# Experts' rows: scaled ahead of the scatter and added in memory, in place of eight stored rows per token

## What is computed

```
_, e_idx = lax.top_k(jnp.where(expert_mask, biased, -jnp.inf), TOP_K)
gate = jnp.take_along_axis(scores, e_idx, axis=1)
gate = gate / jnp.sum(gate, axis=-1, keepdims=True) * ROUTED_SCALE
...
yb = lax.map(expert_block, (xin, block_expert)).reshape(n_rows, d)
routed = jax.ops.segment_sum(yb * row_gate[:, None], row_tok, num_segments=T + 1)[:T]
shared = (jax.nn.silu(hf @ sh_gate) * (hf @ sh_up)) @ sh_down
return (routed + shared).reshape(b, s, d)
```

## Time and profile before

| | us |
|---|---|
| median of 3 runs | 3164.0 (3163.98 to 3166.07) |
| the profiled execution | 3163.8 |
| its span, first to last instruction | 3162.2 |
| TensorE busy | 3057.7 (97%) |
| VectorE busy | 1856.5 (59%) |
| ScalarE busy | 561.5 (18%) |
| GpSimd busy | 245.3 (8%) |
| moved by DMA | 566.57 MB |

### The profile page before, as it was taken

One profiled execution on the slowest core, in us unless ns is written; L12 is line 12 of the kernel. 1 busy time (PEld: TensorE's weight loads), 2 busy tenths in 40 slices (PEclk: granted clock), 3 DMA queues, 4 the chain that ended last, 5 costly groups with the idle time before them and its releaser, 6 DMA issues. The chain is left out here.

```text
span 3162.2 us, 39915 instructions
## 1 busy us (share of the span) xinstructions
PE 3057.7 (97%) x12530; PEld 1759.4 (56%) x12531; DVE 1856.5 (59%) x3939; ACT 561.5 (18%) x1282; POOL 245.3 (8%) x377
## 2 busy tenths in 40 slices
PE   7999999999999899999998898999999999999998
PEld 4765667644437433333333444478844688588543
DVE  6766676666537644334333567665557755665667
ACT  1002222210002122222221225410000233200000
POOL 1000000011100122222222100000000000000000
PEclk9999999999999999999999999999999999999999
DMA  7673232378762479999997521122254334122342
GB/s 224 198 225 95 66 100 60 107 252 274 242 227 100 149 310 384 378 390 402 370 369 274 214 80 54 41 74 102 85 186 160 100 81 134 54 100 80 135 184 106
DMA packets 270692, 566.57 MB, mean 179 GB/s; under 512 B 27017, under 2 KB 162804, under 8 KB 245994
## 3 DMA queue, kind: packets, MB, share of 16 engines
q1 hardware_dynamic: 213712, 413.72, 36.9%
q0 software_dynamic: 46992, 140.43, 12.7%
q10 hardware_dynamic: 9866, 10.82, 1.0%
HBM read 554.22 MB, written 36.83 MB: 187 GB/s over the span
## 5 line engine op out<-in xcount | busy, mean ns | idle before, releaser
L1522 PE MATMUL ps<-WR,hT 128*64 x832 | 373.7, 603 | 22.8 <-issue 20.7
L1523 PE MATMUL ps<-WR,hT 128*64 128x512 f32 x832 | 373.7, 603 | 0.0
L1967 PE MATMUL ps<-WR 128*128 128x512 f32 x784 | 337.4, 592 | 1.0 <-DVEq L3572 0.7
L1522 PEld LDWEIGHTS ps<-WR,hT 128*64 128x64 f32 x832 | 115.2, 139 | 264.9 <-issue 264.9
L1967 PEld LDWEIGHTS ps<-WR 128*128 128x128 f32 x784 | 148.6, 190 | 188.9 <-issue 186.0
L1161 PE MATMUL ps<-hT,WR 128*128 128x512 f32 x512 | 225.5, 596 | 0.6 <-DVE WR L2813 0.6
L3284 DVE COPY WR<-WR 128x1024 f32 x208 | 131.0, 693 | 160.4 <-SPq L756 110.6
L1926 PE MATMUL ps<-WR 128*128 128x256 f32 x960 | 217.0, 379 | 0.0
L1926 PEld LDWEIGHTS ps<-WR 128*128 128x128 f32 x960 | 182.4, 190 | 24.8
L1543 PE MATMUL ps<-WR 128*64 x416 | 189.5, 598 | 2.7 <-DVEq L3297 1.8
L1544 PE MATMUL ps<-WR 128*64 128x512 f32 x416 | 189.7, 598 | 0.0
(11 more groups left out here) (483 smaller groups left out, 4699.3 us busy)
## 6 DMA issues: line engine op xcount, KB each, us to landing
WR<-in_w_gate SPq DMA_DIRECT2D x64, 1024.0 KB, 8.4
WR<-in_w_up SPq DMA_DIRECT2D x64, 1024.0 KB, 10.8
WR<-in_w_down SPq DMA_DIRECT2D x64, 1024.0 KB, 9.9
WR<-in_mlp_w SPq DMA_DIRECT2D x56, 1024.0 KB, 6.8
WR<-in_mlp_w SPq DMA_DIRECT2D x20, 2048.0 KB, 8.4
xr<-in_ada_w POOLq DMA_DIRECT2D x32, 1024.0 KB, 5.6
WR<-in_w_in SPq DMA_DIRECT2D x56, 512.0 KB, 7.0
xr<-in_w_ada POOLq DMA_DIRECT2D x16, 1024.0 KB, 5.6
```

Source lines behind the costliest of these rows:

```text
L1522: mm(out[0:HALF], xT[u][:, k, 0:HALF], wa[:, :, k, :], start=(k == 0), stop=(k == KD - 1))
L1523: last = mm(out[HALF:P], xT[u][:, k, HALF:P], wb[:, :, k, :], start=(k == 0), stop=(k == KD - 1))
L1967: return mm(ps[:, bank, :], rows, weights, start=(row == 0), stop=(row == PAST[phase] - 1))
```

## The change

Each expert's row is multiplied by its gate on the way out of PSUM: `turn_y` takes a scale per row, `gate_c[u]`. The gates of a turn's rows come by one more indirect gather of 128 single numbers from a small array in DRAM, `gate_dram`, which GpSimd writes once ahead of the loop from `gate8`; `pair_i` holds the row numbers for it. The scatter then adds in memory (`compute_op=ALU.add`) to one of four sums per token: by turn parity u (two arrays `y_sums[u]`) and by half of the turn (`half_c` adds 512 to the row number in the upper half). Both arrays are filled with zeros from an input `blank` while the program is still ahead of the routing. The combine stage loads four row tiles per token tile in place of eight, into sixteen places of their own, so that the loads wait for nothing but the last scatters. TensorE adds all four by products with the identity, the shared expert of three tiles goes ahead of the waits, and VectorE reads the sum straight from PSUM. The sixteen products of identity and gate on ScalarE are gone. In the residual of this stage VectorE now does all four `branch_in` first and the four `gained` behind them.

```diff
+        y_sums = [nc.dram_tensor(f"y_sum{u}", (2 * T, D), F32, kind="Internal").ap() for u in range(2)]
+        gate_dram = nc.dram_tensor("gate_dram", (T * PER_TOKEN, 1), F32, kind="Internal").ap()
...
+            for u in range(2):
+                pool.dma_start(y_sums[u].rearrange("(r p) d -> p r d", p=P), blank.unsqueeze(1).to_broadcast(
+                    [P, 2 * TT, D])).then_inc(sem("y_blank"), 16)
...
-            def put(u, column, n):
+            def put(u, column, n, more=True):
...
+                if more:
+                    pool.tensor_copy(pair_c[u].bitcast(I32), pair_i[:, bass.ds(column, 1)].bitcast(I32)).then_inc(
+                        sem("put_c"), 1)
...
+                if more:
+                    pool.indirect_dma_start(gate_c[u], None, gate_dram,
+                                            bass.IndirectOffsetOnAxis(ap=pair_c[u].bitcast(I32), axis=0),
+                                            bounds_check=T * PER_TOKEN - 1, oob_is_err=False).then_inc(
+                                                sem(f"gate_in{u}"), 16)
+                pool.indirect_dma_start(y_sums[u], bass.IndirectOffsetOnAxis(ap=put_c[u].bitcast(I32), axis=0),
+                                        ybuf[u], None, bounds_check=2 * T - 1,
+                                        oob_is_err=False, compute_op=ALU.add).then_inc(sem(f"y_out{u}"), 16)
...
+            pool.wait_ge(sem("route_v"), ROUTE_V["gates"])
+            pool.dma_start(gate_dram.rearrange("(t p j) o -> p t (j o)", p=P, j=PER_TOKEN), gate8).then_inc(
+                sem("gates_out"), 16)
+            pool.wait_ge(sem("gates_out"), 16)
+            pool.wait_ge(sem("y_blank"), 32)
...
+            for t in range(TT):
+                for i in range(ACC):
+                    pool.dma_start(y_in[t][i], y_sums[i // 2][(i % 2) * T + t * P:(i % 2) * T + (t + 1) * P, :]).then_inc(
+                        sem(f"y_in{t}"), 16)
...
+            def ffn_rows(t):
+
+                pe.wait_ge(sem(f"y_in{t}"), 16 * ACC)
+                for i in range(ACC):
+                    for n in range(2):
+                        last = mm(ps[:, 2 * t + n, :], ident[:, :], y_in[t][i][:, 512 * n:512 * n + 512],
+                                  start=False, stop=(i == ACC - 1))
...
+                act.wait_ge(sem(f"gate_in{u}"), (h >> 1) * 16 + 16)
+                A(ybuf[u], ps[:, 5:7, :].rearrange("p b c -> p (b c)"), ACT.Copy, scale=gate_c[u]).then_inc(
+                    sem("moe_y_free"), 1)
...
+            link.mark(V.memset(half_c[0:HALF, :], 0.5 - PER_TOKEN / 2))
+            link.mark(V.memset(half_c[HALF:P, :], 0.5 - PER_TOKEN / 2 + T * PER_TOKEN))
+            for u in range(2):
+                link.mark(V.memset(gate_c[u], 0.0))
...
+            link.mark(V.tensor_copy(pair_i.bitcast(I32), pair))
...
             def combined(t):
...
+                dve.wait_ge(sem("ffn_p"), t + 1)
+                return ps[:, 2 * t:2 * t + 2, :].rearrange("p b c -> p (b c)")
```

More of the change, by code:

```diff
@@ L131 @@
 ROUTE_P = dict(router_p=1, counts_p=2, ranks_p=3, ends_p=4, first_p=5, tiles_p=6, table_p=7, rows_p=8)
-ROUTE_V = dict(chosen=1, before=2, sums=3, starts=4, ends=5, slots=6, tile_e=7, onehot=8, stack=8 + TT, row_i=9 + TT)
+ROUTE_V = dict(chosen=1, before=2, sums=3, starts=4, ends=5, slots=6, tile_e=7, onehot=8, stack=8 + TT, row_i=9 + TT, gates=10 + TT)
 ADA_SHORT = dict(sum=4 + 1, p=1, free=2, into=(0, 0), bufs=2)
@@ L310, with program @@
 ]
-def program(nc, a, onehot, counting, out):
+def program(nc, a, onehot, counting, blank, out):
     ctx = ExitStack()
@@ L476, in program @@
         fold = view(R, 20588, TURNS)
+        pair_i = view(R, 20460, TURNS)
+        pair_c = [view(R, 20524 + i, 1) for i in range(2)]
+        gate_c = [view(R, 20526 + i, 1) for i in range(2)]
+        half_c = view(R, 20528, 1)
         gate8 = view(R, 18724, TT, PER_TOKEN)
@@ L526, in program @@
         modx = view(R, 19968, 9 * ADA_C)
-        yg = [view(R, D * i, D) for i in range(YG)]
-        gate_diag = view(R, 16384, TT * PE_ROWS, P)
+        y_in = [[view(R, D * (ACC * t + i + (1 if t == TT - 1 else 0)), D) for i in range(ACC)] for t in range(TT)]
         ada0 = [view(R, 512 * i, 512) for i in range(4)]
@@ L1580, in ffn_rows @@
                     for k in range(FE):
-                        last = mm(ps[:, 2 * t + n, :], hexp[k][:, t * P:(t + 1) * P], w[:, k, 512 * n:512 * n + 512],
-                                  start=(k == 0), stop=False)
-                last.then_inc(sem("ffn_p"), 1)
[L1584 to L1591, removed]
+                        mm(ps[:, 2 * t + n, :], hexp[k][:, t * P:(t + 1) * P], w[:, k, 512 * n:512 * n + 512],
+                           start=(k == 0), stop=False)
+            def ffn_rows(t):
[4 more added lines that the diff above has]
+                                  start=False, stop=(i == ACC - 1))
+                last.then_inc(sem("ffn_p"), 1)
             have("sh_down", 0)
+            for t in range(TT - 1):
+                shared_rows(t)
             for t in range(TT - 1):
@@ L3061, in residual @@
                     return
-                for t in range(TT + behind):
-                    if t < TT:
+                if branch is not None:
+                    for t in range(TT):
                         branch_in(t)
+                    for t in range(TT):
+                        gained(t)
+                    return
+                for t in range(TT):
+                    branch_in(t)
                     if sums is not None and t == TT - 1:
                         first_sums(sums)
-                    if t >= behind:
-                        gained(t - behind)
+                    gained(t)
             def weight_sums(layer, i):
```

62 lines of the change are left out of this document (16 added, 46 removed).

## The result

| | before, us | changed, us |
|---|---|---|
| median (range, runs) | 3163.99 (3160.24 to 3166.07, 4) | 3182.45 (3180.93 to 3184.39, 4) |
| ratio, 95% interval | | 1.006 (1.0043 to 1.0077) |
| profiled span | 3162.2 | 3182.7 |
| up to the first gate product (L1522, now L1531) | 1060.3 | 1055.8 |
| from there to the first shared product: the loop | 643.7 | 676.0 |

The change makes the kernel 18.5 us slower. The forecast was 3178.0 us, in a range of 3150 to 3212 us. The lower four rows are read from the timelines of TensorE: the loop gives 32.3 us away, the combine stage brings 7.8 us.

The account below looks back on a forecast made before the run. The loop was taken as TensorE's in a normal turn and the DMA engines' at five places. 3163.8 + 29 (loop) + 0.6 (its start) - 15.6 (behind it) = 3178 us; own range 3166 to 3195, stated range 3150 to 3212 us.

Parts of the forecast that it names:

- fourth rival: Loop grows as forecast, but the combine stage gives less or the loop's start is not covered: 3185 us, chance 0.07.
- The add: In each loop turn, the adding scatter costs one more transfer of the same bytes, 0.83 us of DMA time.
- hidden read: Rival: in the loop the add's read costs nothing more, only gate words load the engines: 3153 us, chance 0.25.
- dearer add: Rival: in the loop an adding row takes three transfers' time, or gate packets cost several times more: 3206 us, chance 0.14.
- The gates' words: In each loop turn, gathering the gates' 4-byte numbers, 80 of them valid, costs 0.26 us of DMA time.
- What the loop grows by: 40 middle turns get 43.6 us of DMA work against 24 us free, two thirds filled: +29 us with slow matmuls.
- The waits in the loop: GpSimd's extra issues and ScalarE's wait for the scatter fit in the loop's turns, about 9 us of room left: 0 us.
- landing rival: In the loop scatters land later than about 18 us after issue, so ScalarE's copy waits: 3300 us, chance 0.04.
- The start: At the loop's start, five small VectorE operations ahead of the first gather add 0.6 us; gate store and clearing are covered.
- Behind the loop: In the combine stage, fewer row loads and additions let L1630 start at 1772.7 instead of 1788.3 us: -15.6 us.

Follow-up runs that it names:

- the kernel with neither: The changed kernel with plain writes in place of the adding scatter and without the gate words: 3151.52 us, ratio 0.997 to the kernel before.
- late gains: The kernel before with only VectorE's order in the combine stage changed, the gains behind all four `branch_in`: 3160.27 us, ratio 0.9991.

## Why the prediction was right

The side was right, and the measured 3182.5 us lie 4.5 us from the forecast. The mechanism of the loop was right too, and three of its signs came: more than five late loads with 51.3 us in all (40 to 55 was given), VectorE waiting 179.3 us for SyncE (over 150), and turns of 11.7 us between the stalls.

That the sum came so near is partly luck. In the loop two terms erred against each other, by 6 and by some 8 us. The gain of the combine stage was forecast twice too large. And the profile of the changed kernel has a start that is 4.5 us shorter, which is not the change's; without it the profiled span would be 25 us longer than before and not 20.5. A loop as forecast and a tail that gives less is in its outcome the fourth rival (3185 us, chance 0.07), which lies nearer to the measured time than the forecast does. Its reasons were loads that wait longer than forecast for the last scatter, or an uncovered start, and the rows show neither. One sum was wrong as well: the forecast's own range ends at 3195 us with a gain of 15.6 us behind the loop; with the 12 us that it names it ends at 3198.

- **The add.** One more transfer of the same bytes, 0.83 us a turn. Measured 0.88 to 0.90, and two plain scatters take the same time. The adding scatter takes (0.84 + 0.89) / 0.84 = 2.06 times the engines' time of a plain one. The Trainium skill (Collectives: The Full Stack, The bandwidth ceiling) has 1.93 times a copy for an operation that adds, and puts it down to two source reads on one ring. The number here is near; whether the cause is the same, no run shows. The hidden read (3153 us) and the dearer add (3206 us) both fall: the run with the plain scatter is what a hidden read would have given, 3151 us.
- **The gates' words.** 0.26 us a turn was too much by a factor of five or more; 0.03 to 0.05 was measured. The step that failed divided the landing time of 1024 pieces at the launch by their number, as if that had been the engines' time. Landing includes waiting. The Trainium skill (DMA: Bandwidth & Descriptors, Measured) has about 10.5 ns a packet at the smallest transfer, from which the prediction worked out 0.05 us a turn. That is near the measured time, but not for its reason: the estimate took 80 packets, and the pages count 32. By these a packet costs the engine that carries it 15 to 25 ns (0.03 to 0.05 us x 16 / 32).
- **What the loop grows by.** Forecast +29, of 43.6 us of load with two thirds of 24 us filled, 16 us. Measured +32.3 in the profile, of which 31.9 are late loads, and +29.7 in the medians against the kernel with neither, from 37.3 us of load with some 8 us gone. So too much load (the words) and too much filled made up for each other. The step that failed is that a ring which runs short more often leaves no idle time. It still does: the share reached 0.98 and not the 1.00 to 1.02 that the prediction asked for. A share of 0.98 was its sign of the hidden read; the other sign of that case, stalls below 25 us, did not come.
- **The waits in the loop.** Right: ScalarE never waits for a landing, and GpSimd (1.77 us for issuing an adding scatter, 1.09 for a plain one) has time: from 1084 to 1720 us it still waited 159 us for TensorE and 149 us for ScalarE. The landing rival fell. How late the adding scatters land within the loop no view shows. The two plain ones, whose engines' time is the same, landed after 8.2 and 10.7 us.
- **The start.** Forecast +0.6. TensorE's wait ahead of the first turning grew by 0.4 us (1.32 us, 0.89 before). The 4.5 us in the other direction are not the change's: kernels with the code ahead of the loop as before had their first gate product at 1056.4 us (nine buffers) and 1060.3 us (late gains). About 3 us of it lie in the routing, at another granted clock for the same work. Before, then after:

```profile
1020.00:1030.00 10.00, 9.02 (x60) 8.70 (x59) 5.07 (x27) 0.52 (x1) 0.00 (x0) 0.72 0.13 52
```

```profile
1018.00:1028.00 10.00, 8.93 (x79) 8.21 (x77) 6.12 (x31) 1.12 (x2) 0.00 (x0) 1.00 0.13 52
```

  The store of the gates held GpSimd for 5.5 us, where I had 5, and was covered as forecast. The gather for the third turn went out at 1070.98 us, some 3 us earlier than I had it, but only because the whole start was earlier.

```profile
1063.95 0.83 POOL L972 DMA_DIRECT2D gate_dram<-WR  x1 [9.69 <-DVEq L3331]
...
1070.98 1.05 POOL L941 DMA_INDIRECT hT<-h_dram,WR  x1 [0.88 <-POOLq L940]
```

- **Behind the loop.** Forecast -15.6, measured -7.8 in the profile (-11 in the medians with a plain scatter, where -18 was forecast). Counted from the first shared product, L1642 began at 76.5 us where I had 68.7. The later landing was sized rightly, about 2 us. The step that failed is the adding up of TensorE's chain, in three places. Four row tiles took 8.7 us from issue to use and not 7.5. The eight row products of a tile were put at 8.9 us for the first and 6.4 us for each later tile and took 9.5 and 7.0; the trace of before had 9.71 and 7.13 us already. So the sum of tile 3 ended at 53.4 and not 49. And the index rows of tile 1 ended at 70.3 and not 62: of this 2.6 us are the wait for the turned tile 1, and 1.8 us the slow latent rows behind it. That wait stands in the trace of before too (its timeline has the same 2.56 us ahead of L1602). I had listed TensorE's products there without their waits; with the wait moved, above, the stage takes 71.9 us.

## What to carry to other kernels

An add in the scatter is paid as one more transfer of its rows, in busy time that the count of bytes doesn't show. Here, with the DMA engines already at 0.97 of their time, merging rows in memory cost more in the loop than it saved behind it. Price such a change by the free time that a full prefetch ring lets you use, here a third to a half of what the share suggests. Before changing an algorithm for its last stage, try that stage's own order and buffers: VectorE's new order with nine buffers in place of six made the stage 4.9 us shorter, and three kernels with it were 3.0 to 7.8 us faster. When a chain is timed by adding up an engine's products, take each duration and each wait from the trace, and allow for matmuls behind a wait being slow: 5.41 against 3.62 us here, though not behind every wait.

## What the runs showed of the hardware

The adding scatter: 2.06 times the engines' time of a plain one, 1.77 against 1.09 us of GpSimd for its issue, and 8.3 to 8.7 against 6.1 to 6.8 us from issue to the next instruction at the end of the loop. ScalarE's copy of 128 x 1024 with a scale from a tile takes 1.11 us, with a constant it took 1.03 us. And a gather of 128 single words of 4 bytes is 32 packets and takes 0.03 to 0.05 us of sixteen engines, but 1.08 us of GpSimd for its issue.
